# Local attention's units spread in pieces over its steps, and latent attention's scores as five split products

## What is computed

```python
# 16 query heads of width 64, 4 key heads, 512 tokens in 4 blocks of 128, 16 meta tokens
sc = einsum('bqkgd,bskd->bkgqs', qn, keys)        # keys: 16 meta + up to 256 of the band
p  = sink_softmax(sc, mask, sink)
out = einsum('bkgqs,bskd->bqkgd', p, vals)
merged = sigmoid(g_attn) * attn + sigmoid(g_ssm) * ssm    # q, g_attn, g_ssm come from hn @ w_in
```

```python
s = (einsum('bqhd,bkhd->bhqk', q_nope[:, q0:q1], k_nope[:, :q1])
     + einsum('bqhr,bkr->bhqk', q_rope[:, q0:q1], k_rope[:, :q1])) * scale
pr = softmax(where(mask, s, NEG_INF_2))
outs.append(einsum('bhqk,bkhd->bqhd', pr, v[:, :q1]))
```

## Time and profile before

| what | value |
|---|---|
| median of 3 runs | 2745.61 us (2744.53 to 2750.54) |
| profiled execution | 2743.8 us, its span 2742.0 us |
| PE busy in the span | 98% |
| local attention, scores of item 0 to the last values | 571.86 to 732.65 us |
| latent attention, first scores to the last output | about 1290 to 1580 us |

### The profile page before, as it was taken

One profiled execution on the slowest core, in us unless ns is written; L12 is line 12 of the kernel. 1 busy time (PEld: TensorE's weight loads), 2 busy tenths in 40 slices (PEclk: granted clock), 3 DMA queues, 4 the chain that ended last, 5 costly groups with the idle time before them and its releaser, 6 DMA issues.

```text
span 2742.0 us, 35232 instructions
## 1 busy us (share of the span) xinstructions
PE 2676.6 (98%) x14595; PEld 2244.8 (82%) x14595; DVE 1674.5 (61%) x2553; ACT 1015.2 (37%) x1625; POOL 348.2 (13%) x361
## 2 busy tenths in 40 slices
PE   6999999988899999999999999999999999999999
PEld 6999999866687888887667688888887878888887
DVE  6754755668556544546664667737764467764765
ACT  3321333134334222333442435424454244542435
POOL 1133423020001000011000040000221014000031
PEclk9999999999899999999999999999999999999999
DMA  5243344421132233322111132332322212232231
GB/s 144 77 123 108 104 137 126 167 74 33 33 108 96 92 100 108 89 77 66 43 65 47 58 100 78 90 103 77 114 95 85 85 46 70 85 108 92 90 103 62
DMA packets 292727, 244.02 MB, mean 89 GB/s; under 512 B 19837, under 2 KB 285575, under 8 KB 292567
## 3 DMA queue, kind: packets, MB, share of 16 engines
q1 hardware_dynamic: 282503, 226.40, 26.1%
q0 software_dynamic: 5616, 13.22, 1.6%
q10 hardware_dynamic: 4448, 2.16, 0.3%
HBM read 230.70 MB, written 13.14 MB: 89 GB/s over the span
## 4 chain that ended last, share of the span: by engine, by line
PE 87%; DVE 8%; ACT 2%; issue 1%; DMA 1%; POOL 1%; ACTq 0%; SPq 0%; POOLq 0%; DVEq 0%
PE ps L566 26%; PE ps L567 25%; PE ps L568 25%; PE ps L2320 2%; PE ps L2319 2%; DVE ul L554 2%; PE ps L751 1%; PE ps L2395 1%; DVE rbuf L766 1%; PE ps L2367 1%; ACT S L1786 1%; ACT uh L539 1%; PE ps L3116 1%; PE ps L3092 1%; DVE tmp L2174 1%
## 5 line engine op out<-in xcount | busy, mean ns | idle before, releaser
L554 DVE TENSOR_TENSOR ul<-raw,uh 128x1024 fp32r<-128x1024 f32 (+3 forms) x416 | 526.5, 1289 | 340.5 <-ACT uh L539 340.1
L566 PE MATMUL ps<-OH,uh 128*128 128x512 f32 (+1 forms) x1736 | 646.6, 372 | 3.6 <-DVE ul L554 2.4
L568 PE MATMUL ps<-OH,ul 128*128 128x512 f32 (+1 forms) x1736 | 638.7, 368 | 0.0
L567 PE MATMUL ps<-OL,uh 128*128 128x512 f32 (+1 forms) x1736 | 638.5, 368 | 0.0
L539 ACT CAST uh<-raw 128x1024 fp32r<-128x1024 f32 (+3 forms) x416 | 411.9, 1025 | 158.3 <-PE ps L568 128.6
L566 PEld LDWEIGHTS ps<-OH,uh 128*128 128x128 f32 x1736 | 327.3, 189 | 66.6 <-issue 7.3
L567 PEld LDWEIGHTS ps<-OL,uh 128*128 128x128 f32 x1736 | 327.4, 189 | 55.2 <-issue 2.4
L568 PEld LDWEIGHTS ps<-OH,ul 128*128 128x128 f32 x1736 | 327.3, 189 | 54.6
L566 PE MATMUL ps<-XH,uh 128*128 128x264 f32 (+1 forms) x992 | 314.1, 317 | 13.4 <-DVE ul L554 8.1
L567 PE MATMUL ps<-HL,uh 128*128 128x512 f32 (+2 forms) x946 | 320.3, 339 | 0.0
L566 PE MATMUL ps<-HH,uh 128*128 128x512 f32 (+2 forms) x946 | 320.1, 338 | 0.0
(11 more groups left out here) (434 smaller groups left out, 3710.8 us busy)
## 6 DMA issues: line engine op xcount, KB each, us to landing
raw<-in_ffn_w SPq DMA_DIRECT2D x40, 1024.0 KB, 5.0
raw<-in_ffn_w_up SPq DMA_DIRECT2D x40, 1024.0 KB, 5.0
raw<-in_ffn_w SPq DMA_DIRECT2D x32, 704.0 KB, 4.3
raw<-in_ffn_w_down SPq DMA_DIRECT2D x32, 704.0 KB, 4.3
raw<-in_w_in SPq DMA_DIRECT2D x16, 1024.0 KB, 5.4
raw<-in_gla_w_in SPq DMA_DIRECT2D x12, 1024.0 KB, 5.0
raw<-in_mla_w_o SPq DMA_DIRECT2D x8, 1024.0 KB, 4.8
raw<-in_ple_w_gate SPq DMA_DIRECT2D x8, 1024.0 KB, 4.9
```

The costliest lines, as they stand in the source:

```text
L554: e.tensor_tensor(l, src, h.bitcast(F32), SUB).then_inc(*s_wlo.up(("unit", u)))
L566: e.matmul(o, wh, xh, start=first, stop=False)
L567: e.matmul(o, wh, xl, start=False, stop=False)
L568: return e.matmul(o, wl, xh, start=False, stop=last)
```

## The change

Two edits are made together.

**Local attention.** The 13 units become 104 chunks (one chunk is 3 products). `CHUNKS` says how many are done along each step. A unit that is begun in a step is begun behind the scores; what is left of it comes in the next step between values and transposes. All of them use bank 3, one after the other, and the rest rotates over banks 0 to 2. DVE now gates the values before it normalises; a step in which fewer than 3 chunks are left over (`soon`) puts ACT's turned copies first and DVE's low part of the next unit last.

**Latent attention.** QN, KN and KR are kept as high and low parts. QA holds the rotated queries' high part in one half of the partitions and their low part in the other, so that one product with KRH gives two terms. Each query block takes five float32r products of at least 256 columns. The four swapping copies move from DVE to ACT, and DVE makes QNL, KNL and the low half of QA.

```diff
+        def lin_piece(e, name, X, t0, n, key, bank, k0, k1):
+            xh, xl, tag = X
+            if k0 == 0:
+                piece_of[key] = next_unit(e, name)
+                bk.take(e, key, bank)
+            u = piece_of[key]
+            hi, lo, _ = halves_of(u)
+            for k in range(k0, k1):
+                s_lo.wait_ge(e, (tag, k))
+                i = mm3(e, psum[:, bk.of[key], 0:n], hi[:, k, :], lo[:, k, :], xh[:, k, t0:t0 + n],
+                        xl[:, k, t0:t0 + n], k == 0, k == 7)
+            if k1 == 8:
+                i.then_inc(*s_mm.up(key, ("unit", u)))
...
+        ALONG = [("q" if n < 2 else "ga", 2 * g + n % 2) for g in range(1, 4) for n in range(4)] + [("gs", 0)]
+        CHUNKS = (8, 8, 8, 7, 7, 7, 6, 6, 6, 6, 6, 6, 5, 5, 5, 3, 2, 2, 1, 0)
+        def soon(i):
+            return sum(k1 - k0 for _, k0, k1 in pieces_of(i, True)) < 3
...
         def window_pe(e):
-            bk.limit(4)
+            bk.limit(3)
             for i in range(20):
                 if i >= 4:
                     values_pe(e, i - 4)
-                if q_ga(i):
-                    name, c = q_ga(i)
-                    lin(e, name, MIX, HR, (name, c))
-                if i == 17:
-                    lin(e, "gs", MIX, HR, ("gs", 0))
+                along_pe(e, i, True)
                 if 3 <= i <= 18:
                     turn_pe(e, i - 3)
                 if i < 16:
                     scores_pe(e, i)
+                along_pe(e, i, False)
...
         def window_act(e):
             for i in range(20):
+                if 3 <= i <= 18 and soon(i):
+                    turn_copy(e, i - 3, True)
                 if 1 <= i <= 16:
                     softmax_act(e, i - 1)
-                if q_ga(i - 1):
-                    ga_act(e, *q_ga(i - 1))
-                if q_ga(i):
-                    feed_hi(e, q_ga(i)[0])
+                for name, c in ended(i - 1) if i else ():
+                    ga_act(e, name, c)
+                for name, c in begun(i):
+                    feed_hi(e, name)
-                if 3 <= i <= 18:
+                if 3 <= i <= 18 and not soon(i):
                     turn_copy(e, i - 3, True)
...
         def window_dve(e):
                 if 1 <= i <= 16:
                     softmax_dve(e, i - 1)
+                if i >= 4:
+                    values_dve(e, i - 4)
                 if 2 <= i <= 17:
                     normalise_dve(e, i - 2)
-                if i >= 4:
-                    values_dve(e, i - 4)
-                if q_ga(i):
-                    feed_lo(e, q_ga(i)[0])
+                if not soon(i):
+                    for name, c in begun(i):
+                        feed_lo(e, name)
+                for name, c in ended(i):
+                    (scale the unit's result)
                 if 3 <= i <= 18:
                     turn_copy(e, i - 3, False)
+                if soon(i):
+                    for name, c in begun(i):
+                        feed_lo(e, name)
...
-        def rope_dve(e, key, dst, what):
-            for k in range(4):
-                e.tensor_copy(s[32 * k:32 * k + 32, :], P(key, 512, slice(32 * (k ^ 1), 32 * (k ^ 1) + 32))).then_inc(
+        def rope_act(e, key):
+            for k in range(4):
+                e.copy(rope_tile(key)[32 * k:32 * k + 32, :], P(key, 512, slice(32 * (k ^ 1), 32 * (k ^ 1) + 32))).then_inc(
...
         def queries_act(e, p):
             for hh in range(2):
-                e.copy(QN[:, hh, :], P(("qn", p, hh, 0)))...
-            feed_hi(e, "uk", 1 if p == 1 else 2)
+                e.copy(QNH[:, hh, :], P(("qn", p, hh, 0)))...
+            rope_act(e, ("qr", p, 0))
             for hh in range(2):
-                e.copy(KN[:, hh, :], P(("kn", p, hh, 0)))...
+                e.copy(KNH[:, hh, :], P(("kn", p, hh, 0)))...
+        def queries_turned_act(e, p):              # behind latent_output_act(i - 3)
+            s_dv.wait_ge(e, ("rope", "qr", p, 0))
+            for hh in range(2):
+                rows = slice(64 * hh, 64 * hh + 64)
+                e.copy(QA[rows, hh, :], QR[rows, :]).then_inc(*s_hi.up(("qr", p, hh)))
+            feed_hi(e, "uk", 1 if p == 1 else 2)
...
         def queries_dve(e, p):
+            for hh in range(2):
+                e.tensor_tensor(QNL[hh][:, :], P(("qn", p, hh, 0)), QNH[:, hh, :].bitcast(F32), SUB)...
             rope_dve(e, ("qr", p, 0), QR)
+            for hh in range(2):
+                e.tensor_tensor(KNL[:, hh, :], P(("kn", p, hh, 0)), KNH[:, hh, :].bitcast(F32), SUB)...
+        def queries_turned_dve(e, p):              # behind latent_output_dve(i - 3)
+            for hh in range(2):
+                rows, other = slice(64 * hh, 64 * hh + 64), slice(64 - 64 * hh, 128 - 64 * hh)
+                e.tensor_tensor(QA[other, hh, :], QR[rows, :], QA[rows, hh, :].bitcast(F32), SUB)...
             feed_lo(e, "uk", 1 if p == 1 else 2)
...
         def latent_scores_pe(e, h):
             for n in range(4):
-                N = 128 * (n + 1)
+                N = max(128 * (n + 1), 256)
                 b = bk.take(e, ("ms", h, n), 4 + n)
-                e.matmul(psum[:, b, 0:N], QN[:, hh, 128 * n:128 * n + 128], KN[:, hh, 0:N], start=True, stop=False)
-                e.matmul(psum[:, b, 0:N], QR[p0:p0 + 64, 128 * n:128 * n + 128], KR[p0:p0 + 64, 0:N], start=False,
-                         stop=True).then_inc(*s_mm.up(("ms", h, n), ("ms", h)))
+                o, q = psum[:, b, 0:N], slice(128 * n, 128 * n + 128)
+                mm3(e, o, QNH[:, hh, q], QNL[hh][:, q], KNH[:, hh, 0:N], KNL[:, hh, 0:N], True, False)
+                e.matmul(o, QA[:, hh, q], KRH[:, 0:N], start=False, stop=False)
+                e.matmul(o, QA[:, hh, q], KRL[:, 0:N], start=False, stop=True).then_inc(
```

More of the change, by code:

```diff
@@ L305, in program @@
         misc = m("misc", [128, 16])
+        tmp_at = m.at
         tmps = [m(f"tmp{i}", [128, 528]) for i in range(NTMP)]
@@ L397, in program @@
         CKH, CKL = mL("CKH", [128, 2, 512], F32R), mL("CKL", [128, 2, 512], F32R)
-        KR = Sbuf(nc, acc_at + 5120)("KR", [128, 512])
+        QR, KR = tmps[0][:, 0:512], tmps[3][:, 0:512]
+        KRH, KRL = (Sbuf(nc, tmp_at + 2112 * (1 + i))(n, [128, 512], F32R) for i, n in enumerate(("KRH", "KRL")))
         mO = Sbuf(nc, PH + 16896)
@@ L403, in program @@
         mQ = Sbuf(nc, R1)
-        QR = mQ("QR", [128, 512])
-        QN, KN = mQ("QN", [128, 2, 512]), mQ("KN", [128, 2, 512])
+        KNH, KNL = mQ("KNH", [128, 2, 512], F32R), mQ("KNL", [128, 2, 512], F32R)
+        QA = mQ("QA", [128, 2, 512], F32R)
+        QNL = [Sbuf(nc, at)(f"QNL{i}", [128, 512], F32R) for i, at in enumerate((acc_at + 5120, tmp_at + 3 * 2112))]
         assert mQ.at <= R1 + 12288
@@ L412, in program @@
         zst = mP("zst", [128, 2, 4, 4])
+        QNH = mP("QNH", [128, 2, 512], F32R)
         mX = Sbuf(nc, end_f)
@@ L1727, in spans, with pieces_of, begun, ended @@
             return [(0, 16)] + ([(16 + 128 * (n - 1), 128)] if n else []) + [(16 + 128 * n, 128)]
[L1729 to L1737, removed]
+        ALONG = [("q" if n < 2 else "ga", 2 * g + n % 2) for g in range(1, 4) for n in range(4)] + [("gs", 0)]
+        CHUNKS = (8, 8, 8, 7, 7, 7, 6, 6, 6, 6, 6, 6, 5, 5, 5, 3, 2, 2, 1, 0)
+        def pieces_of(i, rest):
+            a = sum(CHUNKS[:i])
+            b = a + CHUNKS[i]
+            x = [(u, max(a - 8 * u, 0), min(b - 8 * u, 8)) for u in range(len(ALONG)) if a < 8 * u + 8 and b > 8 * u]
+            return [p for p in x if (p[1] > 0) == rest]
+        def begun(i):
+            return [ALONG[u] for u, _, _ in pieces_of(i, False)]
+        def ended(i):
+            x = (pieces_of(i - 1, False) if i else []) + pieces_of(i, True)
+            return [ALONG[u] for u, _, k1 in x if k1 == 8]
+        def soon(i):
+            return sum(k1 - k0 for _, k0, k1 in pieces_of(i, True)) < 3
+        def along_pe(e, i, rest):
+            for u, k0, k1 in pieces_of(i, rest):
+                name, c = ALONG[u]
+                lin_piece(e, name, MIX, 16, 512, (name, c, 0), 3, k0, k1)
         def scores_pe(e, i):
@@ L2214, in latent_first_act @@
             feed_hi(e, "cq")
+            rope_act(e, ("kr", 0))
             root(e, "xk", H2, 1.0 / 256, EPS5)
@@ L2223, in latent_first_act @@
                 e.activation(qsq[c][:, 0:512], CQ[:, c, :], ACT.Square).then_inc(*s_fn.up(("xq", "sq", c)))
+            s_dv.wait_ge(e, "KR")
+            e.copy(KRH[:, :], KR).then_inc(*s_hi.up("KR"))
         def query_norm_act(e):
@@ L2252, in latent_first_dve @@
                     gained_dve(e, "xq", XQ, c - 1, CQ[:, c - 1, :], "mla_q_norm")
+            s_hi.wait_ge(e, "KR")
+            e.tensor_tensor(KRL[:, :], KR, KRH[:, :].bitcast(F32), SUB).then_inc(*s_lo.up("KR"))
         def query_norm_dve(e):
@@ L2492, in latent_act @@
                     latent_output_act(e, i - 3)
+                if i % 2 == 0 and i < 16:
+                    queries_turned_act(e, i // 2)
                 if i == 0:
```

(2 more changed lines are left out.)

56 lines of the change are left out of this document (34 added, 22 removed).

## The result

| what | before | after |
|---|---|---|
| median (runs) | 2745.07 us (2744.43 to 2750.54, 4) | 2696.86 us (2695.48 to 2700.05, 4) |
| profiled span | 2742.0 us | 2694.1 us |
| ratio | | 0.9822 [0.9805, 0.9839] |

The account below looks back on a forecast made before the run. PE, busy 98% of the span, was taken as the bound. From 2743.8 us, latent attention -35 and local attention -14.5 gave 2694.3 us; range 2680 to 2714.

Parts of the forecast that it names:

- A head's scores, 3.20 us: Latent attention: five split products over four column blocks take 3.20 us a head on PE, in place of 5.68.
- The 1.6 us set aside for changes of kind: Latent scores: the first split product behind a float32 one takes 0.2 us more, 8 x 0.2 in all.
- Rival D: Latent scores: weight loads of the five products are not hidden; fully exposed +11 us, 2755; chance 0.02.
- x: Unhidden us of each of 320 latent score weight loads; sum -49.5 + 320x, slower from x = 0.155.
- The layout of a pair, 28.0 us with a wait of 0.75: Latent attention: a pair of heads takes 28.0 us against 32.7, with PE's turn waiting 0.75 for ACT's VT copy.
- Local attention, 146.5 us for the stage: Local attention: 128.1 work + 14 idle + 3 clock = 145, rounded up to 146.5; -14.5 us.
- The stalls in it: Local attention: begun units wait for bank 3: 2.95, 0.25, 1.75, 0.25 (steps 6, 7, 10, 11); 1.05, 1.15, 0.45 (4, 9, 13).
- The drain: Local attention from step 15: few chunks left, values wait for the copies, 0.4 + 0.5 + 3.1 + 0.65 + 0.65 us.
- the unnamed rest: Whole kernel: stalls of another kind, as large as unhidden weight loads; chance 0.02.
- B: Local attention: scaling waits behind a low part, all ten begun units stall PE 1.5 us each; 2709 us, chance 0.14.
- C: Latent attention: DVE and ACT set the pace, 29.5 us a pair instead of 28; 2705 us, chance 0.16.
- the ring: Latent attention: the recurring chain qr, copies, rotation, QA; laid out at 28 us a pair, feared at 29.5.

Follow-up runs that it names:

- the five longer ones: Of nine profiled executions of the changed kernel, its unaltered copy and kernels unchanged in this stage, the five whose local attention took 156.1 to 156.4 us.
- the kernel with 13 whole pieces: Changed kernel with CHUNKS set so 13 local attention steps have a whole unit and 7 none; 2703.86 us, ratio 0.9856.
- The three-product kernel: Changed kernel with two of the five latent score products (nope high by low, QA by KRL) left out; 2692.10 us, ratio 0.9822.

## Why the prediction was right, point by point

**What bounds the kernel.** Right: PE's own stream. The gain is PE's busy time (-44.0) and its gaps, while DVE and ACT each do more than before.

**A head's scores, 3.20 us.** Measured 3.23, with 0.12, 0.12, 0.173 to 0.18 and 0.23 us from start to start. The middle taken for 384 columns was right to 0.005. PE's work in the stage fell by 42.3 us (313.7 to 271.4) where 38.1 was summed. The scores themselves give what was said, 2.46 us a head for 2.48: from start to start 5.77 us before (1348.04 to 1353.81) and 3.31 after (1325.77 to 1329.08). The 1.6 us set aside for changes of kind were too much: such a change costs 0.08 in front of a head's scores (0.20 to the next start, where the later ones take 0.12), and the queries behind save 0.11 of it in every pair, 0.4 in all. The rest lies in the transposes and output products of a pair, which take 0.2 us less beside split products.

**Rival D and the weight loads.** Each of the twenty products of a head has a weight load in the trace, and the ten of 256 columns still start 0.12 us apart, so x is next to nothing and D is out. The Trainium skill, "TensorE: Matmul & The Clock Gate", in the mechanism of Part 3, has loads overlap only with products of other row groups; the estimate by it put 34 us on top and the kernel at 2728. It came at 2696.86, and the head at 3.23 leaves no room for it.

**The layout of a pair, 28.0 us with a wait of 0.75.** Measured 27.73 with a wait of 0.82, of the releaser that was named. It comes four times, not six: 3.3 us where 4.5 were summed.

**What was missed in latent attention.** Three waits in steps that the layout of a middle pair doesn't hold, and the clock. The first pair: KRH, KRL, KNL and QA came late for the first scores, 1.4 + 1.6 = 3.0 us where the text had 1 at worst. The last values: PE waits 2.27 us for OL at 1524.14, where the 1.7 us of such waits were counted as saved; they rose to 3.0. A third is smaller: a low weight part is 1.4 us late for the projection in step 10. So the waits grew by 6.8 where 4.5 - 1.7 = 2.8 was summed, 4 us too few. And the sum has no term for the clock in this stage. It lost 5.1 us, over 1269 to 1276 and, behind the wait of 2.27, over 1525 to 1529; before it lost 1.7, and nothing in the kernel with the local change alone. The work fell by 4.2 more than summed. -42.3 + 6.8 + 3.4 = -32.1 in place of -35.3: the misses in the waits and the clock are more than half hidden by the one in the work.

**Local attention, 146.5 us for the stage.** The gain was near, -13.7 against -14.5, and this was in good part luck. The forecast counted its layout from the end of the scores of item 0 and compared it with the length of before from that moment, 571.86. The first unit stands in front of them there and behind them after, so the layout held a unit of 5.65 us more than the 160.79 us that it was set against. And it was too short: the stage takes 152.7 us from there where 146.5 was said. Against the like length of before, 166.4, the layout claimed 19.9 and 13.7 came. By the terms: idle 11.1 where about 14 was said, clock 3.1 where 3 was, and work 138.5 against the 128.1 of before; 5.7 of that difference is the unit, 4.7 is new and was put at nothing. The clock's 3 is met in the execution compared here; in the five longer ones it is some 6, and the gain of the stage only some 11. Of the 4.7, the first split product behind plain float32 scores costs 0.34 us to the next start where it costs 0.23 otherwise:

```profile
632.03 0.50 PE L570 MATMUL ps<-XH,uh 128*128 128x512 f32 x1
632.37 0.39 PE L571 MATMUL ps<-XL,uh 128*128 128x512 f32 x1
```

That is 0.11 us a change of kind, which was counted for the latent scores and left out here: 1.5 us for the 14 changes more, and the kernel with 13 whole pieces has about 1 less of work. What the other 3.5 us or so are stays open.

**The stalls in it.** Steps 6 and 10: 2.95 and 1.75 said, 2.41 and 2.27 measured, in the two places named and released by the scaling named. The experiment that puts the low part last took both away, so that mechanism is shown and not only read off. The three small ones in steps 4, 9 and 13 came as two of 0.6 to 0.74 us. The drain: 5.9 said, some 4.8 measured. The clock fell behind both large ones, as said.

**The whole.** 2694 forecast, 2696.86 measured; 2.1 us of the gain lie outside both stages, where the sum has nothing. That the total is nearer than its terms is chance. The named chances for a gain add to 0.97 with half of the unnamed rest, not to the 0.95 given.

**Rivals.** B had all ten units stall on bank 3: four did (Q and Mg above), 6.0 us in place of 15. C was set at 0.16. It had the ring come round in 29.5 us. The three-product kernel shows the ring at 27.07, under the 27.73 that PE needs, but by 0.66 only.

## What to carry to other kernels

When one engine sets the pace and a change makes its work cheaper, lay out the ring of the others from one release to the next as well, and not only how busy they are: here DVE was at 81% and ACT at 60% of a pair, and yet the ring left 0.66 us. An instruction that waits for another engine delays all that is queued behind it, so put it last, or into a stretch where its engine is idle; putting it later in a full stretch costs more than the wait that it removes. Before the lengths of a stage in two kernels are compared, both stretches must hold the same work; the count of records shows it (793 and 793 here). And a stage's length contains the falls of the clock of that one execution, so compare several, or take idle time, clock and work apart.

## What was new of the hardware

- The distance from start to start of a split product hardly shrinks below 256 columns: 0.12 us at 256, and still 0.11 at 128.
- The length of one wait doesn't decide on TensorE's clock. In the kernel after, the granted clock fell to the lower level behind waits of 2.41 and 2.27 us, and behind one of 1.53 at 719.76 that follows two of 0.77 (the windows of 1 us from 720 to 723 are at 0.50); it did not behind one of 1.67 at 706.98 (705 to 710 is at 1.00), but behind the same wait it did in the kernel with the local change alone (706 to 712). In the kernel before it fell behind 1.91.
- The same wait can cost different amounts. Behind the wait of 2.41 us the clock was low over 620 to 624 in the kernel after, 1.7 us lost, and over 618 to 629 in the control, which is the same kernel, 5.1 us lost.
- A split product of 512 columns takes 0.34 us from its start to the next behind plain float32 products, and 0.23 behind its own kind.
- A copy out of PSUM on ACT takes no less time for fewer partitions. The swapping copies of 32 partitions by 512 columns took 0.58 us each on the mean, four in 2.38, and the casts of 128 partitions by 512 columns 0.58 to 0.59:

```profile
1316.17 2.38 ACT L2218 COPY tmp<-ps 32x512 f32<-32x512 f32 x4 [0.72 <-PE ps L572]
```
